# Rounding and subtracting the weights of the chunked products a whole slot of four contraction tiles at a time

## What is computed

```python
proj = h @ w_in[l]                                   # 2048 x 5456
x = x + g1 * (merged @ w_out[l])                     # 2048 x 2048
u = h @ w_up                                         # 2048 x 11008
uc = conv_b + sum(up[:, i:i + S] * conv_w[i] for i in range(3))
gate, val = jnp.split(uc, 2, axis=-1)
return (jax.nn.silu(gate) * val) @ w_down            # 5504 x 2048
...
for l in range(2):                                   # second block
    proj = jnp.einsum('bsd,dn->bsn', _rms_norm(x, norm_g[l]), w_in_2[l])   # 2048 x 6726
    ...                                              # three kinds of attention
    x = x + jnp.einsum('bsm,md->bsd', mixed, w_out_2[l])
```

## Time and profile before

| | |
|---|---|
| median of 3 runs | 2447.41 us (2442.9 to 2450.64) |
| the profiled execution's own time | 2442.12 us |
| its span, first to last instruction | 2440.3 us, 28115 instructions |
| mean granted TensorE clock | 0.957 of full speed |
| busy: TensorE / VectorE / ScalarE / GpSimd | 89% / 67% / 47% / 11% |
| `lo` (L249, VectorE) | 694 instructions, 861.3 us busy |
| `hi` (L241, ScalarE) | 694 instructions, 698.1 us busy |

### The profile page before, as it was taken

How to read it: one execution, slowest core, us unless ns; L and a number is a source line. 1 busy time by engine, 2 the same in 40 slices (tenths; PEclk the granted TensorE clock), 3 DMA queues, 4 the chain that set the end, 5 groups by cost and what they waited for, 6 DMA issues and landing times.

```text
span 2440.3 us, 28115 instructions
## 1 busy us (share of the span) xinstructions
PE 2160.6 (89%) x10018; PEld 1791.9 (73%) x10018; DVE 1631.0 (67%) x2191; ACT 1142.4 (47%) x1668; POOL 277.6 (11%) x208
## 2 busy tenths in 40 slices
PE   0589996597999999997999989998779999997887
PEld 0468885476777788886888878887558888886666
DVE  4878886596799888886676654455456644464555
ACT  1224335544544444444455544465465544563554
POOL 0000001011222223222020200001101100001100
PEclk9989998798999999998999999999889999998888
DMA  7869991095677655555556455543215555542143
GB/s 277 340 246 335 361 365 44 4 349 207 233 259 251 205 189 178 183 164 181 193 178 191 164 177 187 177 153 130 86 52 173 193 189 183 169 166 74 50 139 120
DMA packets 237367, 458.50 MB, mean 188 GB/s; under 512 B 12414, under 2 KB 184652, under 8 KB 236748
## 3 DMA queue, kind: packets, MB, share of 16 engines
q1 hardware_dynamic: 235928, 455.96, 53.7%
q10 hardware_dynamic: 1332, 1.14, 0.1%
HBM read 454.95 MB, written 2.10 MB: 187 GB/s over the span
## 4 chain that ended last, share of the span: by engine, by line
PE 66%; DVE 8%; ACT 5%; issue 4%; POOL 1%; DVEq 0%; ACTq 0%
PE PS L253 20%; PE PS L255 19%; PE PS L254 19%; DVE WLO L249 2%; PE PS L965 2%; PE PS L908 2%; DVE AD L310 1%; ACT WHI L241 1%; PE PS L973 1%; PE PS L1085 1%; DVE BIG L1376 1%; DVE WK L1117 1%; DVE WK L1102 1%; ACT BIG L675 0%; PE PS L980 0%
## 5 line engine op out<-in xcount | busy, mean ns | idle before, releaser
L253 PE MATMUL PS<-WHI,HH 128*128 128x512 f32 (+2 forms) x2752 | 1088.8, 396 | 78.7 <-DVE WLO L249 72.1
L249 DVE TENSOR_TENSOR WLO<-RAWT,WHI 128x1024 fp32r<-128x1024 f32 (+4 forms) x694 | 861.3, 1252 | 344.1 <-ACT WHI L241 343.0
L255 PE MATMUL PS<-WHI,HLO 128*128 128x512 f32 (+2 forms) x2752 | 1071.0, 389 | 0.0
L254 PE MATMUL PS<-WLO,HH 128*128 128x512 f32 (+2 forms) x2752 | 1070.4, 389 | 0.0
L241 ACT ACTIVATE WHI<-RAWT 128x1024 fp32r<-128x1024 f32 (+4 forms) x694 | 698.1, 1016 | 503.2 <-PE PS L255 474.1
L253 PEld LDWEIGHTS PS<-WHI,HH 128*128 128x128 f32 x2752 | 525.1, 191 | 194.9 <-issue 66.1
L255 PEld LDWEIGHTS PS<-WHI,HLO 128*128 128x128 f32 x2752 | 524.8, 191 | 102.6
L254 PEld LDWEIGHTS PS<-WLO,HH 128*128 128x128 f32 x2752 | 525.6, 191 | 98.4 <-issue 1.0
L310 DVE SCALAR_TENSOR_TENSOR AD<-AD,SM 128x1024 f32<-128x1024 f32 x86 | 127.6, 1484 | 5.2 <-DMA AD<-w_ada 2.6
L613 ACT ACTIVATE HH<-BIG 128x256 fp32r<-128x256 f32 x118 | 48.9, 415 | 131.8 <-PE PS L255 130.9
L617 DVE TENSOR_TENSOR HLO<-BIG,HH 128x256 fp32r<-128x256 f32 x118 | 55.7, 472 | 41.1 <-ACT HH L613 41.1
(11 more groups left out here) (287 smaller groups left out, 1569.3 us busy)
## 6 DMA issues: line engine op xcount, KB each, us to landing
RAWT<-w_in SPq DMA_DIRECT2D x104, 960.0 KB, 4.7
RAWT<-w_up SPq DMA_DIRECT2D x168, 512.0 KB, 4.6
AD<-w_ada SPq DMA_DIRECT2D x152, 512.0 KB, 5.6
RAWT<-w_out SPq DMA_DIRECT2D x96, 512.0 KB, 4.7
RAWT<-w_down SPq DMA_DIRECT2D x86, 512.0 KB, 4.4
RAWT<-w_in SPq DMA_DIRECT2D x44, 992.0 KB, 7.6
BIG<-w_ada SPq DMA_DIRECT2D x40, 512.0 KB, 7.9
RAWT<-w_in SPq DMA_DIRECT2D x8, 972.0 KB, 4.8
```

What stands on the lines that cost most here:

```text
L249: dve.tensor_tensor(WLO[:, (q % HL) * GR:(q % HL) * GR + size], r, h.bitcast(F32), ALU.subtract)\
L253: pe.matmul(o, lh, wh, start=first, stop=False)
L254: pe.matmul(o, lh, wl, start=False, stop=False)
L255: return pe.matmul(o, ll, wh, start=False, stop=last)
```

## The change

In chunks whose product has four slots (`ph.spc == 4`: w_in, w_up and w_in_2), ScalarE rounds a whole slot with one ACTIVATE (`hi_slot`) and VectorE subtracts a whole slot with one TENSOR_TENSOR (`lo_slot`). The semaphores rise by 2 for a slot. `hi_slot` waits for `mm_done` >= q - 2 with q = 2gs, so it may start when TensorE has finished the whole slot gs - 2. The hooks of both halves of a slot now stand before the slot's one instruction. TensorE's code is unchanged and still waits half by half.

```diff
+        def hi_slot(act, gs, reg, per_slot, size):
+            q = 2 * gs
+            act.wait_ge(raw_in[gs % RAW], reg * per_slot + uses[gs])
+            ge(act, S("mm_done"), reg * 2 + (q - 2))
+            o = (q % HL) * GR
+            act.activation(WHI[:, o:o + 2 * GR].rearrange("p (j c) -> p j c", j=2)[:, :, 0:size],
+                           raw_slot(gs)[:, 0:2 * size].rearrange("p (j c) -> p j c", j=2), ACT.Copy)\
+               .then_inc(S("hi_done"), 2)
+
+        def lo_slot(dve, gs, reg, size):
+            q = 2 * gs
+            dve.wait_ge(S("hi_done"), reg * 2 + (q + 2))
+            o = (q % HL) * GR
+            part = [t[:, o:o + 2 * GR].rearrange("p (j c) -> p j c", j=2)[:, :, 0:size] for t in (WHI, WLO)]
+            dve.tensor_tensor(part[1], raw_slot(gs)[:, 0:2 * size].rearrange("p (j c) -> p j c", j=2),
+                              part[0].bitcast(F32), ALU.subtract).then_inc(S("lo_done"), 2)
...
                 for j in range(2):
                     if before and 2 * s + j in before:
                         before[2 * s + j](act)
-                    hi(act, gs, reg, 8 if ph.gates else 4, j, ph.kg * (n or ph.n))
+                    if ph.spc < 4:
+                        hi(act, gs, reg, 4, j, ph.kg * (n or ph.n))
+                if ph.spc == 4:
+                    hi_slot(act, gs, reg, 8 if ph.gates else 4, ph.kg * (n or ph.n))
...
                 for j in range(2):
                     if before and 2 * s + j in before:
                         before[2 * s + j](dve)
-                    lo(dve, gs, reg, j, ph.kg * (n or ph.n))
+                    if ph.spc < 4:
+                        lo(dve, gs, reg, j, ph.kg * (n or ph.n))
+                if ph.spc == 4:
+                    lo_slot(dve, gs, reg, ph.kg * (n or ph.n))
```

## The result

The changed kernel takes 2612.7 us, median of 4 runs (2607.44 to 2615.86), against 2449.0 (2442.9 to 2450.95) for the kernel before on the same chip: ratio 1.0671, 95% interval 1.0642 to 1.0699, some 164 us slower. The profiled execution took 2607.44 us, its span 2605.6.

What follows compares the result with a forecast made beforehand. TensorE, busy 89% of the span, was taken as the bound; added lateness of 92 + 25 + 5 + 20 + 4 = 146 us on the profiled 2442.1 gave 2588, stated as 2592, range 2530 to 2645.

Steps and rivals of the forecast that it cites:

- ten plain chunk intervals: w_up intervals between exponentials without w_ada work: 27.3 us against 22.85, costing 45 us in all.
- six with w_ada: w_up intervals where a w_ada multiply-add of 1.2 us joins the loop: 28.5 against 24.17, 26 us in all.
- two boundaries: After w_up's chunks 5 and 9, reciprocal and lo_slot follow TensorE's reduction: 6.8 us each with the loop, 14 together.
- end of w_up: Chunk 20 +5.6, chunk 21 +2.4, the taps behind it +1.5: 9.5 us together.
- first chunk of w_up: The alternating chain of conversions and splits gets shorter per slot but starts later: -2 us.
- w_in_2: heads: First two chunks of w_in_2, both layers: activation splits and statistics come before whole slots, +20 us.
- w_in_2: softmax and transposes: Beside chunks 10 to 13, softmax waits cost 25 us over both layers, the second layer's transposes 5.
- clock, by itself: TensorE's slow matmuls behind new waits, in w_up largely covered by VectorE's 6.7 us: +4 us.
- Fewer, longer instructions: In 232 slots of w_in, w_up and w_in_2, merging saves 0.04 and 0.06 us per slot, costed at nothing.
- w_up's loop: Chunks 1 to 21: exponential, hi_slot, lo_slot, reciprocal, next lo_slot, TensorE's H0 to H2 and tap sum to 27.3 us.
- Covered in w_up: Rival, chance 0.08: GpSimd slows a long lo_slot no further, loop 25.0 us; with w_in_2 estimates too high by half, 2522.
- half rate after every new wait: Rival, chance 0.07: each of some 40 TensorE waits costs 1.6 us of uncovered slow matmuls, +64, 2656 us.

Runs made afterwards that it cites:

- the mended kernel: Changed kernel, w_up chunks 1 to 19 with exponential and reciprocal behind the slot instructions, halves in fully hooked and first chunks: 2452.7 us, ratio 1.0041.
- the filler: Changed kernel plus ten unused TensorE matmuls ahead of the wait for half 6 in w_up's chunks 1 to 19: 2592.1 us, ratio 1.0603.

## Why the prediction was right, and where its steps failed

The forecast was 2592 us, range 2530 to 2645; measured 2612.7. The cause it named is the cause: long instructions that wait at the head of an in-order engine behind a hook that only concerns their second half. Moving the hooks in one part of the places and halving the instructions in the rest gives 94% back. Term by term, measured from the exponentials of both traces and the ratios:

| term | forecast, us | measured, us |
|---|---|---|
| ten plain chunk intervals | +45 | +44 (4.4 each) |
| six with w_ada | +26 | +19 (3.2 each) |
| two boundaries | +14 | +18.4 (37.8 and 37.7 against 28.75 and 28.37) |
| end of w_up | +9.5 | +12.4 (chunk 20 alone 8.3) |
| first chunk of w_up | -2 | +10.7 |
| w_in_2: heads | +20 | +25 |
| w_in_2: softmax and transposes | +30 | +36 |
| clock, by itself | +4 | in the rows above |

**Fewer, longer instructions: nothing.** Right. With free slots merged the ratio is 1.0045, no gain; in the mended kernel plain chunks are as long as before, 22.87 us. The Trainium skill's rule that larger is better (VectorE: DVE Perf Modes, The TRN2 errata) shows in single durations (a pair of `lo` 2.34 us, one `lo_slot` 2.28) and in no run's time.

**w_up's loop.** The total of 27.3 was right, two of its terms were not. "`lo_slot` 2.28, plus what GpSimd costs it: ... 1.2" measured 0.57, and "plus 1.1 beside L1133" measured 0. I spread the slowdown of the earlier trace rows in proportion to the overlap. The rows after show exclusion: whichever begins later stands until the other's instruction has ended. With one long `lo_slot` VectorE loses only the rest of GpSimd's instruction, and where it is first, nothing. The Trainium skill states this (SBUF — State Buffer, SBUF: two separate sides): a VectorE instruction with two SBUF inputs and a GpSimd instruction that reads SBUF use a shared port pair as an exclusive lock, and whichever starts first has it for its whole instruction. The traces agree: a `lo_slot` that came second took 3.33 us instead of 2.28, GpSimd's addition 2.61 instead of 1.30. One row agrees only in part: GpSimd's multiply L1159 began 0.26 us after a `lo_slot` and ended 1.17 us after that one's end, although it takes 2.06 alone, so by that estimate some 0.9 us of it was not held back. That page would have corrected the term; I had not weighed it.

The rival *Covered in w_up* had this condition, and it nearly held (0.6 us of GpSimd's 2.3 were left). The chunk still did not fall to its 25.0, since TensorE's slow matmuls took VectorE's place in the loop.

**The clock, "+4".** This is the step that failed. I had slot 3 at half rate "largely covered by VectorE's 6.7 us". With VectorE's chain 1.7 us shorter than summed, TensorE's slow slot was the longer one and set the loop: 1.5 us in each plain chunk, shown by the filler (27.3 to 25.8) and by the reciprocal, whose move out of the chain did nothing there. The rival of half rate after every new wait was wrong in its other half: in w_in_2 the waits of 0.98 and 1.36 us were followed by full speed, and of seven between 1.85 and 2.03 us only three were followed by slow matmuls.

**With w_ada, 28.5.** Wrong by 1.1, from the same error: the multiply-add lies in VectorE's chain, which has that much room under TensorE's slow slot.

**Boundaries.** Forecast by the loop, +6.8; measured +9.1 and +9.3. Against the kernel before, the new wait for half 6 is 2.6 us and the slow matmuls behind it 1.5; the wait at the boundary is 6.30 and 6.09 us instead of 2.04 and 1.83, and eleven or twelve matmuls are slow behind it instead of eight, 0.6 us. That adds up to 9.0, and the 2.1 of slow matmuls are what the sum left out:

```profile
902.70 0.80 PE L273 MATMUL PS<-WHI,HH 128*128 128x512 f32 x1 [6.09 <-DVE WLO L269]
```

**First chunk, "-2".** Wrong in sign. I took it as one chain of ScalarE and VectorE that gets shorter, and left out TensorE's transposes behind its own halves, although the table of hooks names them: tile 3 comes behind half 0, and slot 1 now needs it. Per slot the distance of the roundings rose from 8.08 to between 9.5 and 11.6 us, and the chunk with its approach costs 10.7.

**End of w_up.** Chunk 21 and the taps behind it were forecast well (2.4 and 1.5 us; measured 2.6 and 1.6). Chunk 20 cost 8.3 instead of 5.6; with halves it takes its 23.7 us again, but which of its waits were mis-sized is left open.

**w_in_2.** The softmax waits were forecast well. TensorE's waits of the first heads in the first layer:

```profile
1727.61 0.49 PE L273 MATMUL PS<-WHI,HH 128*128 128x480 f32 x1 [1.86 <-DVE WLO L269]
...
1741.29 0.48 PE L273 MATMUL PS<-WHI,HH 128*128 128x480 f32 x1 [1.36 <-DVE WLO L269]
...
1755.28 0.48 PE L273 MATMUL PS<-WHI,HH 128*128 128x480 f32 x1 [0.98 <-DVE WLO L269]
```

They read 1.86, 1.36 and 0.98 where the prediction had 2.2, 1.65 and 1.35; all seven of the layer sum to 10.3 (12.5), in the second layer too. The waits for the transposes of the second layer are 1.61, 1.59 and 2.03 (1.5, 1.65 and 2.2 in the forecast). That makes 10.3 of the 14.5 us by which this stretch grew in the first layer, and 15.5 of 21.3 in the second. Some of the rest is slow matmuls, behind one wait of the first layer and two of the second; it was not separated further. The heads come to 25 us (20).

**What was to show it.** 230 halves and 232 slot forms are there, plain chunks of w_in_2 keep their length, and w_up's plain chunks take 27.3 us. The wait for half 6 is 2.6 us and not over 3, and the 1.1 us before the next half 0 is not there; the slow matmuls take their place.

**The rule against the change.** The Trainium skill (Perfetto Trace Analysis, Optimizing Scalar/DVE Operations) has it that engines that are not saturated but cause bubbles elsewhere may finish sooner with their instructions broken up. That was the better guide here: with `lo` or `hi` back in halves, the plain chunk fell from 27.3 to 24.7 or 24.5. The runs add a condition: with hooks placed behind, the plain chunk of w_up loses nothing by length.

## What to carry to other kernels

Before merging two instructions of an in-order engine, list everything that is issued between them and ask who waits for the first half alone; if something urgent stands there, put it behind the merged instruction or leave the pair. Follow such a chain through every engine, the bottleneck too: a wait on TensorE costs its length and, when the clock falls, the slow matmuls behind it, so two mergings that alone cost 1.8 and 1.7 us a chunk cost 4.4 together. Where VectorE sets the pace, as beside w_ada here, place GpSimd's work beside its one-input instructions: that alone was worth 0.2%, and the merging nothing.

## What the runs showed of the hardware

- **Clock.** In w_up, behind waits of 1.34 to 1.59 us TensorE took 5.6 us for the next 24 matmuls. Behind 2.57 to 2.67 it took 6.9 to 7.2 in each of the 17 such places of the changed kernel where no second wait followed within the 24, some eight matmuls being 0.43 us apart. Behind 2.00 to 2.10, and in w_in_2 behind 1.85 to 2.03, both happened. Ten small matmuls of no use in the wait (2.39 us) kept the clock at 1.00 and made the kernel about 17 us faster, by the ratios.
- **VectorE and GpSimd** exclude each other instruction by instruction when VectorE reads two tiles from SBUF: a `lo_slot` of 2.28 us took 3.33 behind a GpSimd product, a GpSimd copy of 16 elements 2.27 behind a `lo_slot`. Beside the reciprocal, which reads one, GpSimd's product took its plain 1.30.
